# Retention in four chunks with a carried state instead of one causal square, inside a hybrid mixer on one Trainium2 core

## The reference, cut to what matters

```
decay  = where(rel >= 0, exp(log_gamma * rel), 0)          # rel = t - s inside a chunk
scores = einsum('bhncd,bhnsd->bhncs', q, k) * decay
o_intra = einsum('bhncs,bhnsv->bhncv', scores, v)
kv = einsum('bhncd,bhncv->bhndv', k * k_decay, v)          # one state's growth per chunk
o = einsum('bhcd,bhdv->bhcv', q_n, state) * q_decay
state = state * chunk_decay + kv_n                         # from chunk to chunk
```

## Time and profile before

| | us |
|---|---|
| median of 3 runs (lowest, highest) | 2417.52 (2414.93, 2419.92) |
| the profiled execution, its time | 2420.88 |
| its span, first to last instruction | 2419.1 |
| TensorE matmuls busy in the span | 2335.3 (97%) |
| VectorE / ScalarE / GpSimd busy | 1651.3 / 663.9 / 183.2 |
| stretch from the first retention scores to the last retention values | 225.46 to 253.49 |

### The profile page before, as it was taken

One profiled execution on the slowest core, in us unless ns is written; L12 is line 12 of the kernel. 1 busy time (PEld: TensorE's weight loads), 2 busy tenths in 40 slices (PEclk: granted clock), 3 DMA queues, 4 the chain that ended last, 5 costly groups with the idle time before them and its releaser, 6 DMA issues.

```text
span 2419.1 us, 35289 instructions
## 1 busy us (share of the span) xinstructions
PE 2335.3 (97%) x14624; PEld 1898.2 (78%) x14624; DVE 1651.3 (68%) x2569; ACT 663.9 (27%) x1200; POOL 183.2 (8%) x179
## 2 busy tenths in 40 slices
PE   8998879999999999999989999999999999999997
PEld 6886668878888888887756788888888888888886
DVE  6674366756888865559788777666667886666653
ACT  2321253022211201324768413222102113222200
POOL 0001222001000011003211010000010000000000
PEclk9999579999999999999999999999999999999998
DMA  4220003412222453322200361232562451322341
GB/s 183 79 79 2 21 3 122 158 52 88 96 96 96 135 204 130 107 81 92 88 1 2 138 219 62 98 100 97 197 214 104 182 186 63 102 96 96 127 141 64
DMA packets 71728, 253.94 MB, mean 105 GB/s; under 512 B 8560, under 2 KB 8848, under 8 KB 71056
## 3 DMA queue, kind: packets, MB, share of 16 engines
q1 hardware_dynamic: 71280, 251.14, 30.4%
q10 hardware_dynamic: 288, 0.54, 0.1%
HBM read 247.97 MB, written 2.10 MB: 103 GB/s over the span
## 4 chain that ended last, share of the span: by engine, by line
PE 47%; DVE 3%; issue 0%; ACT 0%; POOL 0%; DVEq 0%; POOLq 0%
PE psum L393 14%; PE psum L394 14%; PE psum L395 13%; PE psum L3362 1%; PE psum L487 1%; PE psum L3349 1%; PE psum L3384 1%; DVE scratch L3440 1%; DVE scratch L3416 1%; PE psum L656 0%; PE psum L3376 0%; PE psum L465 0%; DVE h L534 0%; DVE n L530 0%; PE psum L476 0%
## 5 line engine op out<-in xcount | busy, mean ns | idle before, releaser
L393 PE MATMUL psum<-rounded_n,rounded_high 128*128 128x512 f32 x1824 | 722.1, 396 | 8.0 <-DVE rounded_ring L346 4.6
L394 PE MATMUL psum<-rounded_n_low,rounded_high 128*128 128x512 f32 x1824 | 712.1, 390 | 0.0
L395 PE MATMUL psum<-rounded_n,rounded_ring 128*128 128x512 f32 x1824 | 712.0, 390 | 0.0
L346 DVE TENSOR_TENSOR rounded_ring<-ring,rounded_high 128x1024 fp32r<-128x1024 f32 (+1 forms) x360 | 448.4, 1246 | 43.5 <-ACT rounded_high L329 31.5
L393 PEld LDWEIGHTS psum<-rounded_n,rounded_high 128*128 128x128 f32 x1824 | 343.9, 189 | 86.6 <-issue 7.4
L394 PEld LDWEIGHTS psum<-rounded_n_low,rounded_high 128*128 128x128 f32 x1824 | 344.1, 189 | 74.2 <-issue 3.9
L395 PEld LDWEIGHTS psum<-rounded_n,rounded_ring 128*128 128x128 f32 x1824 | 343.7, 188 | 72.1
L344 DVE CAST rounded_high<-ring 128x1024 fp32r<-128x1024 f32 (+1 forms) x347 | 250.4, 722 | 188.3 <-PE psum L395 177.9
L393 PE MATMUL psum<-rounded_arena,rounded_high 128*128 128x512 f32 x720 | 280.2, 389 | 0.0
L395 PE MATMUL psum<-rounded_arena,rounded_ring 128*128 128x512 f32 x720 | 280.1, 389 | 0.0
L394 PE MATMUL psum<-rounded_arena,rounded_high 128*128 128x512 f32 x720 | 280.1, 389 | 0.0
(11 more groups left out here) (507 smaller groups left out, 2798.3 us busy)
## 6 DMA issues: line engine op xcount, KB each, us to landing
ring<-in_w_up SPq DMA_DIRECT2D x132, 512.0 KB, 3.6
ring<-in_w_down SPq DMA_DIRECT2D x48, 512.0 KB, 3.5
n_low<-in_mod_w SPq DMA_DIRECT2D x48, 512.0 KB, 5.8
arena<-in_mod_w SPq DMA_DIRECT2D x48, 512.0 KB, 5.3
ring<-in_w_ab_in SPq DMA_DIRECT2D x37, 512.0 KB, 3.6
ring<-in_w_mix_in SPq DMA_DIRECT2D x31, 512.0 KB, 3.6
ring<-in_w_sc_in SPq DMA_DIRECT2D x24, 512.0 KB, 5.7
ring<-in_w_down SPq DMA_DIRECT2D x24, 384.0 KB, 3.0
```

The costliest lines, as they stand in the source:

```text
L346: nc.vector.tensor_tensor(self.rounded(raw), raw, self.rounded(high), ALU.subtract).then_inc(self.weights_split, 1)
L393: self.nc.tensor.matmul(out, w_high, x_high, start=first, stop=False)
L394: self.nc.tensor.matmul(out, w_high, x_low, start=False, stop=False)
L395: return self.nc.tensor.matmul(out, w_low, x_high, start=False, stop=last)
```

## The change

Retention is written in four chunks of 128 tokens. `ret_scores(m)` now makes only the four diagonal squares of both heads of a tile (8 products of 128 columns), and there are two such calls in place of eight. The tables of decay over 512 tokens become one mask of 128 columns for each head. The queries are scaled in place by a table of token and head (two GpSimd multiplications, new semaphore `ret_queries`). The keys are transposed to token-major (`turn(KEYS_TURN)`), VectorE scales them (`ret_tails`), TensorE forms the growth of the state of chunks 0 to 2 (`ret_grow`, 12 products of 64 columns), VectorE carries the state (`ret_grown_states`), and `ret_values(m)` adds, for each chunk, state times queries and values times weights. All of it is placed anew in the lists of the engines.

```diff
...
     freqs = (np.float32(10000.0) ** (-np.arange(0, HD, 2, dtype=np.float32) / HD)).astype(np.float32)
     c["freq"] = freqs[part % (HD // 2)][:, None]
     log_gamma = np.log(1.0 - np.exp2(-5.0 - np.arange(HEADS)))
-    rel = tok[None, :] - part[:, None]
-    for h in range(HEADS):
-        c[f"decay{h}"] = np.where(rel >= 0, np.exp(log_gamma[h] * np.maximum(rel, 0)), 0.0) * HD ** -0.5
+    local = np.arange(P)
+    owner = np.repeat(log_gamma, HD)
+    c["ret_mask"] = np.concatenate([np.where(local[None, :] >= part[:, None], np.exp(-log_gamma[h] * (part[:, None] + 1)), 0.0)
+                                    for h in range(HEADS)], axis=1)
+    c["ret_query"] = np.concatenate([np.exp(owner[m * P:(m + 1) * P, None] * (local[None, :] + 1)) * HD ** -0.5
+                                     for m in range(2)], axis=1)
+    c["ret_tail"] = np.exp(owner[None, :] * (P - 1 - part[:, None]))
+    c["ret_whole"] = np.exp(owner.reshape(2, P).T * P)
     s, t = part[:, None] % 32, np.arange(32)[None, :]
     small = [(s // (2 * b) == t // (2 * b)) & (s % (2 * b) < b) & (t % (2 * b) >= b) for b in LEVELS[:5]]
     c["small_masks"] = np.concatenate([m * 1.0 for m in small + [s == t]], axis=1)
...
     uses = [(0, s) for s in range(DIAG, VALUES + 1)]
     uses += [(1, s) for s in (DIAG, 0, 1, 2, 3, CROSS_A, 4, CROSS_B, BIG)]
     uses += [(2, s) for s in (DIAG, 0, 1, 2, 3, CROSS_A, 4, CROSS_B, BIG, VALUES)]
-    TURNS, RETS = 2, 8
+    TURNS, KEYS_TURN = 3, 2
 
     def use_at(u, s):
         return TURNS + uses.index((u, s))
...
                 pe.wait_ge(taken, x)
             else:
                 pe.wait_ge(weighted, 1)
-            for i in range(4):
-                t, g = (RV, BV, CV, DI)[2 * x + i // 2], i % 2
+            for i in range(4 if x < KEYS_TURN else 2):
+                t, g = (RV, BV, CV, DI, RK)[2 * x + i // 2], i % 2
                 for q in range(4):
                     last = nc.tensor.transpose(
-                        k.psum[:, G0 + i, q * P:(q + 1) * P],
+                        k.psum[:, G0 + i + (2 if x == KEYS_TURN else 0), q * P:(q + 1) * P],
                         z[:, t + q % 2, (2 * g + q // 2) * P:(2 * g + q // 2 + 1) * P], k.const("ident"))
             last.then_inc(filled, 1)
 
...
                                             z[rows, BQ + m, cols], start=True, stop=True)
             last.then_inc(paired, 1)
 
-        def ret_scores(i):
-            m, j = divmod(i, TT)
-            if i == 0:
-                pe.wait_ge(taken, TURNS)
-            elif i == 1:
+        def ret_scores(m):
+            if m == 0:
+                pe.wait_ge(taken, KEYS_TURN)
+            else:
                 pe.wait_ge(weighted, 4)
-            else:
-                pe.wait_ge(ret_weighted, 2 * i - 2)
-            for s in range(2):
-                rows = head_rows(s)
-                last = nc.tensor.matmul(k.psum[:, RET_BANK[i % 2] + s, 0:T - j * P], z[rows, RK + m, j * P:(j + 1) * P],
-                                        z[rows, RQ + m, j * P:T], start=True, stop=True)
+            pe.wait_ge(ret_queries, m + 1)
+            for c in range(TT):
+                cols = slice(c * P, (c + 1) * P)
+                for s in range(2):
+                    rows = head_rows(s)
+                    last = nc.tensor.matmul(k.psum[:, RET_BANK[m] + s, cols], z[rows, RK + m, cols],
+                                            z[rows, RQ + m, cols], start=True, stop=True)
             last.then_inc(ret_scored, 1)
 
-        def ret_values(i):
-            m, j = divmod(i, TT)
-            pe.wait_ge(ret_weighted, 2 * i + 2)
-            for s in range(2):
-                h = 2 * m + s
-                last = nc.tensor.matmul(k.psum[head_rows(s), G0 + 2 + m, j * P:T],
-                                        k.v_tok[:, 0, j, h * HD:(h + 1) * HD],
-                                        k.ret_w[2 * (i % 2) + s][:, 0:T - j * P],
-                                        start=(j == 0), stop=(j == TT - 1))
+        def ret_grow():
+            pe.wait_ge(taken, TURNS)
+            pe.wait_ge(ret_weighted, 1)
+            for c in range(TT - 1):
+                for h in range(HEADS):
+                    at, own = HD * (2 * c + h // 2), slice(h * HD, (h + 1) * HD)
+                    last = nc.tensor.matmul(k.psum[head_rows(h), G0, at:at + HD], k.ret_keys[:, c, own],
+                                            k.v_tok[:, 0, c, own], start=True, stop=True)
+            last.then_inc(ret_grown, 1)
+
+        def ret_values(m):
+            pe.wait_ge(ret_weighted, 2 * m + 2)
+            pe.wait_ge(ret_states, 1)
+            for c in range(TT):
+                cols = slice(c * P, (c + 1) * P)
+                if c >= 1:
+                    for s in range(2):
+                        rows = head_rows(s)
+                        nc.tensor.matmul(k.psum[rows, G0 + 2 + m, cols], k.ret_state[rows, c - 1, m, :],
+                                         z[rows, RQ + m, cols], start=True, stop=False)
+                for s in range(2):
+                    h = 2 * m + s
+                    last = nc.tensor.matmul(k.psum[head_rows(s), G0 + 2 + m, cols],
+                                            k.v_tok[:, 0, c, h * HD:(h + 1) * HD], k.ret_w[h][:, cols],
+                                            start=(c == 0), stop=True)
             last.then_inc(ret_mixed, 1)
 
         def piecewise(out, keys, values):
...
         query_products(1)
         inverse_times(2)
         ret_scores(0)
+        inverse_update(2)
+        turn(KEYS_TURN)
+        inverse_times(3)
         ret_scores(1)
-        inverse_update(2)
+        inverse_update(3)
+        ret_grow()
+        inverse_times(4)
+        inverse_update(4)
         ret_values(0)
-        ret_scores(2)
-        inverse_times(3)
+        join_first()
         ret_values(1)
-        ret_scores(3)
-        inverse_update(3)
-        ret_values(2)
-        ret_scores(4)
-        ret_values(3)
-        ret_scores(5)
-        inverse_times(4)
-        ret_values(4)
-        ret_scores(6)
-        inverse_update(4)
-        ret_values(5)
-        ret_scores(7)
-        ret_values(6)
-        join_first()
-        ret_values(7)
         join_second()
         use(0)
         join_third()
...
         nc.gpsimd.memset(k.diag[:], 0.0).then_inc(cleared, 1)
         nc.gpsimd.memset(k.comp[:], 0.0).then_inc(cleared, 1)
         nc.gpsimd.memset(k.inv_t[:], 0.0).then_inc(cleared, 1)
-        pool.wait_ge(filled, TURNS)
+        for m in range(2):
+            scale = k.const("ret_query")[:, m * P:(m + 1) * P].unsqueeze(1).broadcast_to([P, TT, P])
+            nc.gpsimd.tensor_tensor(blocks(z[:, RQ + m, :]), blocks(z[:, RQ + m, :]), scale, ALU.mult
+                                    ).then_inc(ret_queries, 1)
+        pool.wait_ge(filled, KEYS_TURN)
         nc.gpsimd.memset(k.x11[:], 0.0).then_inc(cleared, 1)
         for t in range(AHEAD):
             difference(t)
...
             link(nc.vector.tensor_tensor(k.xt, k.xt, k.psum[:, D0 + 1, :], ALU.subtract))
             nc.vector.transpose(k.xn, k.xt).then_inc(inverse, 1)
 
-        def ret_weight(i):
-            m, j = divmod(i, TT)
-            dve.wait_ge(ret_scored, i + 1)
-            if i >= 2:
-                dve.wait_ge(ret_mixed, i - 1)
+        def ret_weight(m):
+            dve.wait_ge(ret_scored, m + 1)
             for s in range(2):
-                nc.vector.tensor_tensor(k.ret_w[2 * (i % 2) + s][:, 0:T - j * P],
-                                        k.psum[:, RET_BANK[i % 2] + s, 0:T - j * P],
-                                        k.const(f"decay{2 * m + s}")[:, 0:T - j * P], ALU.mult
+                h = 2 * m + s
+                mask = k.const("ret_mask")[:, h * P:(h + 1) * P].unsqueeze(1).broadcast_to([P, TT, P])
+                nc.vector.tensor_tensor(blocks(k.ret_w[h]), blocks(k.psum[:, RET_BANK[m] + s, :]), mask, ALU.mult
                                         ).then_inc(ret_weighted, 1)
+
+        def ret_tails():
+            dve.wait_ge(filled, TURNS)
+            nc.vector.tensor_tensor(
+                k.ret_keys, k.psum[:, G0 + 2:G0 + 4, :].rearrange("p a (b x) -> p (a b) x", x=2 * P),
+                k.const("ret_tail").unsqueeze(1).broadcast_to([P, TT, 2 * P]), ALU.mult).then_inc(taken, 1)
+
+        def ret_grown_states():
+            dve.wait_ge(ret_grown, 1)
+            grown = k.psum[:, G0, 0:6 * HD].rearrange("p (c m x) -> p c m x", m=2, x=HD)
+            link(nc.vector.tensor_copy(k.ret_state[:, 0, :, :], grown[:, 0, :, :]))
+            for c in (1, 2):
+                for m in range(2):
+                    step = nc.vector.scalar_tensor_tensor(k.ret_state[:, c, m, :], k.ret_state[:, c - 1, m, :],
+                                                          k.const("ret_whole")[:, m:m + 1], grown[:, c, m, :],
+                                                          ALU.mult, ALU.add)
+                    if m == 0 or c == 1:
+                        link(step)
```

(15 more changed lines are left out.)

10 lines of the change are left out of this document (6 added, 4 removed).

## The result

The changed kernel took 2421.4 us (median of 20 runs, 2418.2 to 2427.45) against 2416.93 us (20 runs, 2414.93 to 2421.61) for the kernel before on the same chip: a ratio of 1.0022 [1.0014, 1.003], slower by 0.22%. That is 5.4 us above the forecast and 0.9 us above the end of the range. The times of the changed kernel lie in two groups, 12 runs up to 2422.3 us and 8 from 2425.1 us on; the profiled execution, 2427.09 us, is of the second.

The account below looks back on a forecast made before the run. TensorE bounds the kernel, and in the small-product stage its instruction count in pages of 256; eight pages save 1.5 us, other terms nothing, from the 2417.5 median to 2416.0 us; 8-in-10 range 2409.5 to 2420.5.

Parts of the forecast that it names:

- Pages of 256 instructions: TensorE's list arrives in blocks of 256 instructions, in the small-product stage each taking at least about 3.6 us; eight to `join_third`.
- rival A: Pages don't hold and only the chain counts: `join_second` starts 10.5 us earlier, 2407 us; chance 0.20.
- the chain's check: Whether data arrives in time from `inverse_times(3)` to `use(0)`: at full clock it does, so `join_third` starts at 256.9.
- The sum: Eight pages at 3.6 us, 28.8 to 29.1 us, put `join_third` at 256.9 instead of 258.44: gain 1.5 us.
- rival B: Clock falls near 235 and stays half: `join_third` 2.6 us later, 2420.1; as much again in scans and norms, 2422.7; chance 0.19.
- by ratio: Values of one tile, scaled by column pairs from L1646's 1.16 us: 1.8 us at full clock, 3.6 at half.
- The forecast gain: `join_third` starts 1.5 us earlier, passed on to the end because TensorE's list is in order and busy behind the stage.
- VectorE, GpSimd, tables: Weights, key scaling, states (at most 3.6 us), query scaling, semaphores and smaller tables hide behind other work: counted at nothing.

Follow-up runs that it names:

- b_pad: Kernel before with the third inverse chain product made twice, 256 instructions and 1.3 us of work more; 2422.1 us, ratio 1.0015.
- b_wide: Kernel before with two added products of 128x128 by 512 columns, 8 instructions, ahead of `inverse_times(3)`; 2419.33 us, ratio 1.0.
- b_narrow: Kernel before with all retention products and weights cut to 128 columns, same instructions, off-diagonal blocks left out of the output; 2422.05 us, ratio 1.0007.
- b_split: Kernel before with score and value products cut into pieces of 128 columns, 192 instructions more, same columns; 2420.8 us, ratio 1.0007.
- a_warm: Changed kernel plus four unused products of 512 columns on the inverse chain, to hold the clock up; 2423.95 us, ratio 1.0016.
- a_spread: Changed kernel with weighted values moved forward onto the inverse chain, only state products left in `ret_values`; 2416.32 and 2417.48 us, ratios 0.9991 and 0.9989.
- a_grouped: Changed kernel with each tile's state-times-query products first and the weighted values behind, instead of by turns; 2418.87 us, ratio 1.0001.
- a_again: The changed kernel as it is, measured and profiled a second time; 2423.19 us, ratio 1.002 to the kernel before.

## Why the prediction was wrong

**Pages of 256 instructions: right in the main, and the count exact.** Eight pages lie between the boundary in `inverse_update(2)` and `join_third`. b_pad and b_wide show the rule from both sides: 256 instructions with 1.3 us of work cost 3.4 us, 8 instructions with 1.9 us of work cost none that the trace shows. With that rival A falls. The rule has an exception that the prediction missed, the page of 5.9 us in b_narrow and b_wide, and b_split doesn't fit it. The Trainium skill ("Runtime: NRT & Kernel Launch", "Instruction fetch mechanics") calls the crossing "mostly hidden"; b_pad's page of 3.73 us around 1.27 us of work disagrees, and the measurement decides.

**The step that failed is the last one of the chain's check: "So at full clock the pages decide and `join_third` starts at 256.9".** The comparison holds, as a_warm shows: at full clock the last three pages take 3.65 us each. What failed is the condition. A page time is a least time. The sum took 3.6 us for every page, also for the two that hold the values, `join_first` and `join_second`, and so put the half clock at nothing; it stood only in rival B, at 0.19. At 0.50 the work of both was longer than that: 6.62 and 6.33 us, and the eighth 3.02. The three came to 15.97 us, 5.1 more than three times 3.6 (10.8 to 10.9) and 5.0 more than in a_warm, and that is nearly the whole miss at `join_third`: 38.04 us behind `inverse_times(2)` against 32.7 forecast (256.9 less 224.24). It fits the whole result, too: `join_third` moved by +3.8 and +4.9 us in two traces, the median by +4.5. That the one makes the other isn't shown by a_warm, whose whole time did not fall.

**Two terms in it.** First the clock. The values of one tile take 2.6 us at full clock in a_warm and 4.4 at half. Second the turning between two shapes, a term that the prediction did not have at all: it took 1.8 and 3.6 us "by ratio" from L1646, which has one shape. Grouped by shape the 28 matmuls take 3.4 us at half clock and, in a_spread, 1.8 at full, so the ratio was good and the order was not. By turns they take 0.8 us more than the prediction's figure at either clock. The turning costs time only while the clock is down: at full clock it fitted into the page waits of a_warm. At half, a_grouped took 14.25 us for the three pages in place of 15.97, with the clock back for a part of them.

**Where the gain went.** The forecast gain is in the trace: 2.00 us up to update 4 (1.3 in a_again). Behind it, the kernel before had 16 of its retention matmuls left, three calls of values and one of scores, in 4.66 us. Its five other calls of values lay between the chain's pieces, where b_narrow shows that their columns cost nothing. The change put all 56 matmuls of values behind update 4, in the one place of the stage where no page wait hides them, 10.51 us long. a_spread, which moves a part of that forward and sorts it, recovers the loss; since its clock was up as well, the place, the order and the clock are not told apart there.

**Rival B had the right mechanism and the right sign, but not the moment.** It decided on a clock still down at 246, and on 0.50 from 235 to beyond 251. The clock was down, came back, and fell again at 247.19, just ahead of the values, to stay at 0.50 until 298.39:

```profile
236.95:243.78 6.83, 5.60 (x169) 5.06 (x169) 3.23 (x5) 0.00 (x0) 0.00 (x0) 0.50 0.02 5
243.78:247.19 3.41, 1.49 (x128) 1.31 (x128) 1.91 (x4) 0.00 (x0) 0.00 (x0) 1.00 0.02 5
```

It had values 1 end at 255.5, 31.3 us behind `inverse_times(2)`; they ended 33.2 behind it, 0.8 us for each tile's turning and the rest ahead of the values. It had `join_third` 2.6 us late, and it was 3.8 and 4.9. Its second half, the same loss once more in the scans and norms, did not come: behind `join_third` the changed kernel was 2.5 and 9.1 us shorter than before, and that part was 105 to 115 us long in kernels which have nothing changed in it. Its number, 2422.7, is near the result for another reason than it gave.

**VectorE, GpSimd, tables: nothing, as said.** The waits shown above hold no more than 1.1 us for VectorE. The states took 1.5 us on VectorE (3.6 at most by the prediction) and were there before the values asked for them. What lies behind the stage, from `mix_out` to TensorE's last matmul, is 2032.65 to 2034.20 us in all thirteen traces.

**What stays open.** Up to `inverse_times(2)` the changed kernel took 18.79 and 17.89 us from the first product of the stage, before 16.09. But b_wide, whose list there is the one of before, took 17.62, and a_grouped, whose list is the changed one, 16.60. Over all traces it is 16.09 to 17.62 in the five kernels with the list of before and 16.35 to 18.79 in the eight with the changed one, 0.8 us apart in the mean. I don't count it to the change, but up to that much may belong to it. Why the clock was up behind update 4 in a_spread and down in a_grouped isn't settled, nor whether a_warm gives its gain back or only hides it.

## What to carry to other kernels

Where TensorE runs hundreds of small products, list its instructions by 256 and ask of each page which is longer, its fetch or its work: work placed in a page that waits is free, the same work a page further on costs its full length, and at half clock that is nearly twice what the full-clock rows say (3.4 us against 1.8 for a tile's values, grouped). Fewer columns buy nothing in a page that waits (b_narrow). More instructions can cost a whole page (b_pad) and need not (b_split). Before a change takes wide products out of a stage, ask what they were covering, and lay what replaces them into the same gaps, sorted by kind.
